# Prompt attention: the scores' float32 products become three products of float32r halves, and ScalarE's order of copies and exponentials is turned round

## The reference, cut to what matters

```python
s = jnp.einsum('nqgrd,nqkgd->nqgrk', qb.astype(jnp.float32), k_g.astype(jnp.float32)) * (HEAD_DIM ** -0.5)
s = jnp.where(valid[:, :, None, None, :], s, -jnp.inf)
p = jax.nn.softmax(s, axis=-1)
o = jnp.einsum('nqgrk,nqkgd->nqgrd', p, v_g.astype(jnp.float32))
```

## Time and profile before

| | |
|---|---|
| median of 3 runs | 2370.66 us (2369.03 to 2371.35) |
| profiled execution, its own time | 2368.82 us |
| its span in the trace | 2365.5 us |
| attention block, first product to last | 491.0 to 662.8 us |
| TensorE, VectorE, ScalarE, GpSimd busy over the span | 95%, 42%, 33%, 27% |

### The profile page before, as it was taken

The page is one execution under the profiler, slowest core; times in us unless marked ns, Lnnn a source line. Parts: engine busy times, 40 slices in busy tenths (PEclk is TensorE's granted clock), DMA queues, the critical chain, the costliest instruction groups (busy, mean ns, idle before and its releaser), DMA issues. The chain is left out here.

```text
span 2365.5 us, 37220 instructions
## 1 busy us (share of the span) xinstructions
PE 2237.6 (95%) x13836; PEld 2057.6 (87%) x13836; DVE 1002.6 (42%) x2441; ACT 781.3 (33%) x1414; POOL 633.8 (27%) x387
## 2 busy tenths in 40 slices
PE   5998899699989999999999999888999999999998
PEld 4885489355579999999999999888999999999998
DVE  2525789776435433333332332457333333323323
ACT  4203578645534312212212212354122122121124
POOL 4110111257735222222222222432222222222224
PEclk8997999789999999999999999899999999999999
DMA  8454373500032111111111111101111111111112
GB/s 304 138 171 123 112 254 117 169 28 1 1 127 80 54 46 45 45 53 44 44 44 44 44 53 54 37 20 45 45 45 45 44 46 51 45 44 44 44 44 82
DMA packets 208668, 170.29 MB, mean 72 GB/s; under 512 B 14477, under 2 KB 202109, under 8 KB 208565
## 3 DMA queue, kind: packets, MB, share of 16 engines
q1 hardware_dynamic: 201917, 154.64, 21.0%
q10 hardware_dynamic: 4160, 8.65, 1.0%
q0 software_dynamic: 2496, 5.77, 1.0%
HBM read 155.85 MB, written 11.64 MB: 71 GB/s over the span
## 5 line engine op out<-in xcount | busy, mean ns | idle before, releaser
L525 PE MATMUL pair<-hhi,whi 128*128 128x352 f32 x2184 | 716.2, 328 | 29.7 <-DVE hlo L726 8.5
L526 PE MATMUL pair<-hlo,whi 128*128 128x352 f32 x2184 | 704.9, 323 | 0.0
L527 PE MATMUL pair<-hhi,wlo 128*128 128x352 f32 x2184 | 704.6, 323 | 0.0
L2193 POOL TENSOR_TENSOR wlo<-wraw,whi 128x1024 fp32r<-128x1024 f32 x127 | 304.4, 2397 | 1145.3 <-ACT whi L2138 1144.1
L525 PE MATMUL pair<-hidh,whi 128*128 128x352 f32 x1536 | 495.4, 323 | 0.0
L526 PE MATMUL pair<-hidl,whi 128*128 128x352 f32 x1536 | 492.7, 321 | 0.0
L527 PE MATMUL pair<-hidh,wlo 128*128 128x352 f32 x1536 | 492.2, 320 | 0.0
L537 DVE SCALAR_TENSOR_TENSOR x<-pair,mod,x 128x352 f32<-128x352 f32 (+1 forms) x432 | 247.3, 573 | 513.6 <-PE pair L527 512.6
L525 PEld LDWEIGHTS pair<-hhi,whi 128*128 128x128 f32 x2184 | 412.4, 189 | 40.7 <-issue 19.2
L526 PEld LDWEIGHTS pair<-hlo,whi 128*128 128x128 f32 x2184 | 413.5, 189 | 0.4
L527 PEld LDWEIGHTS pair<-hhi,wlo 128*128 128x128 f32 x2184 | 412.2, 189 | 0.5
(11 more groups left out here) (287 smaller groups left out, 1964.4 us busy)
## 6 DMA issues: line engine op xcount, KB each, us to landing
wraw<-in_w_up_dram SPq DMA_DIRECT2D x64, 512.0 KB, 3.9
wraw<-in_w_down_dram SPq DMA_DIRECT2D x64, 512.0 KB, 3.4
mraw_i<-in_w_mod_dram SPq DMA_DIRECT2D x20, 1024.0 KB, 5.8
mraw_q<-in_w_mod_dram SPq DMA_DIRECT2D x12, 1024.0 KB, 5.1
mraw<-in_w_mod_dram SPq DMA_DIRECT2D x8, 1024.0 KB, 9.3
wraw<-in_dsa_w_in_dram SPq DMA_DIRECT2D x16, 512.0 KB, 5.9
mraw_w<-in_w_mod_dram SPq DMA_DIRECT2D x8, 1024.0 KB, 5.1
wraw<-in_dsa_w_o_dram SPq DMA_DIRECT2D x16, 512.0 KB, 4.0
```

What stands on the lines that cost most here:

```text
L525: pe.matmul(out, a, hi[:, kr, r], start=(n == 0), stop=False)
L526: pe.matmul(out, a, lo[:, kr, r], start=False, stop=False)
L527: last = pe.matmul(out, b, hi[:, kr, r], start=False, stop=(n == len(ks) - 1))
L2193: pool.tensor_tensor(wlo[:, slot(k), :], wraw[:, slot(k), :], whi[:, slot(k), :], ALU.subtract).then_inc(lo_ready, 1)
```

## The change

The scores of t = 1 to 7 are made of three float32r products (upper query · upper key, upper query · lower key, lower query · upper key) in place of one float32 product. A piece is at least 256 columns wide. For this the halves have to exist: `SPLITS` lists 18 of them (14 of a group of four query heads, 4 of 256 key columns for both key heads, each 128 x 512 elements), placed in rounds h = 1, h = 2 (keys) and h = 4 of the stage before they are used. ScalarE writes the upper half behind the exponential of that round, and VectorE waits for it (`q_upper`) and writes the lower half behind its reciprocal. TensorE waits for `q_rest` at the first head of a group. Tile t = 0 stays as it was. ScalarE's round becomes the copies of n - 3 and then the exponential of n.

```diff
+        KW2 = 2 * P
+        SPLITS = []
+        for t in range(1, TILES):
+            n = HEADS * (t - 1)
+            SPLITS.append((n + 1, "q", t, 0))
+            if t % 2 == 0 or t == 1:
+                SPLITS.append((n + 2, "k", t // 2, None))
+            SPLITS.append((n + 4, "q", t, 1))
+        SPLIT0 = 2 * len(IDX_TILES)
...
+                    if h % GROUP == 0:
+                        pe.wait_ge(q_rest, SPLIT0 + splits_needed(t, h))
+                    a, b = qh[:, t % 2, h, :], ql[:, t % 2, h, :]
                     for s in range((L + 511) // 512):
-                        w = min(512, L - 512 * s)
-                        ins = pe.matmul(pair[1 + n % 2][:, s, 0:w], qt[:, h, t * P:(t + 1) * P],
-                                        kt[:, h // GROUP, 512 * s:512 * s + w], start=True, stop=True)
+                        w = max(KW2, min(512, L - 512 * s))
+                        r = slice(512 * s, 512 * s + w)
+                        out = pair[1 + n % 2][:, s, 0:w]
+                        pe.matmul(out, a, kh[:, h // GROUP, r], start=True, stop=False)
+                        pe.matmul(out, a, kl[:, h // GROUP, r], start=False, stop=False)
+                        ins = pe.matmul(out, b, kh[:, h // GROUP, r], start=False, stop=True)
...
                 for n in range(N + AHEAD):
+                    if n >= AHEAD:
+                        copies(n - AHEAD)
                     if n < N:
                         L = P * (qk_list[n][0] + 1)
                         act.wait_ge(neg_done, n + 1)
...
-                    if n >= AHEAD:
-                        copies(n - AHEAD)
+                    for at_n, kind, i, half in SPLITS:
+                        if at_n == n:
+                            whole, upper, _ = split_parts(kind, i, half)
+                            act.activation(upper, whole, ACT.Copy).then_inc(q_upper, 1)
...
                     if 1 <= n <= N:
                         recip(n - 1)
+                    for m, (at_n, kind, i, half) in enumerate(SPLITS):
+                        if at_n == n:
+                            whole, upper, lower = split_parts(kind, i, half)
+                            dve.wait_ge(q_upper, SPLIT0 + m + 1)
+                            dve.tensor_tensor(lower, whole, upper, ALU.subtract).then_inc(q_rest, 1)
```

More of the change, by code:

```diff
@@ L303, in hybrid_step @@
         pt = [put("pt0", [P, TILES, GROUP * P]), at("pt1", [P, TILES, GROUP * P], F32, whi.manual_sbuf_range[0])]
-        assert pt[0].manual_sbuf_range[1] <= s1 and pt[1].manual_sbuf_range[1] <= wlo.manual_sbuf_range[1]
+        kh, kl = (put(n, [P, KV, SEQ], F32R) for n in ("kh", "kl"))
+        qh, ql = (put(n, [P, 2, HEADS, P], F32R) for n in ("qh", "ql"))
+        assert ql.manual_sbuf_range[1] <= s1 and pt[1].manual_sbuf_range[1] <= wlo.manual_sbuf_range[1]
         pair = [ctx.enter_context(nc.psum_tensor(f"pair{i}", [P, 2, 512], F32)) for i in range(4)]
@@ L1839, in hybrid_step, with split_parts, splits_needed @@
         PV_AFTER = AHEAD + GROUP
+        KW2 = 2 * P
[7 more added lines that the diff above has]
+        SPLIT0 = 2 * len(IDX_TILES)
+        def split_parts(kind, i, half):
+            if kind == "q":
+                h = slice(GROUP * half, GROUP * (half + 1))
+                return qt[:, h, i * P:(i + 1) * P], qh[:, i % 2, h, :], ql[:, i % 2, h, :]
+            c = slice(KW2 * i, KW2 * (i + 1))
+            return kt[:, :, c], kh[:, :, c], kl[:, :, c]
+        def splits_needed(t, h):
+            return max(m for m, (_, kind, i, half) in enumerate(SPLITS)
+                       if (kind == "q" and i == t and half == h // GROUP) or (kind == "k" and i <= t // 2)) + 1
         with nc.Block() as block:
@@ L1856, in qk @@
                     L = P * (t + 1)
-                    for s in range((L + 511) // 512):
-                        w = min(512, L - 512 * s)
-                        ins = pe.matmul(pair[1 + n % 2][:, s, 0:w], qt[:, h, t * P:(t + 1) * P],
-                                        kt[:, h // GROUP, 512 * s:512 * s + w], start=True, stop=True)
+                    if t == 0:
+                        pe.matmul(pair[1 + n % 2][:, 0, 0:P], qt[:, h, 0:P], kt[:, h // GROUP, 0:P], start=True,
+                                  stop=True).then_inc(qk_ready, 1)
+                        return
+                    if h % GROUP == 0:
+                        pe.wait_ge(q_rest, SPLIT0 + splits_needed(t, h))
+                    a, b = qh[:, t % 2, h, :], ql[:, t % 2, h, :]
+                    for s in range((L + 511) // 512):
+                        w = max(KW2, min(512, L - 512 * s))
[4 more added lines that the diff above has]
+                        ins = pe.matmul(out, b, kh[:, h // GROUP, r], start=False, stop=True)
                     ins.then_inc(qk_ready, 1)
```

## The result

The changed kernel takes 2397.49 us (median of 4, 2389.73 to 2398.49), the kernel before 2371.01 us in the same comparison: a ratio of 1.0096, 95% interval 1.0073 to 1.0119. It is slower by about 1%, where 2374.4 us had been forecast with 2381 as the upper end. A second comparison gave 2388.83 against 2371.68 us, ratio 1.0085 (1.0064 to 1.0105).

A forecast was written before the change was run, and what follows sets the result against it. TensorE was taken to bound the block from t = 4 on, VectorE the early stages once halves are added. Stage differences summed to +3.7 us on the 2370.66 us median, giving 2374.4 us, range 2366 to 2381.

The forecast's parts named there:

- The price of a half: On VectorE each half costs the exponential + 0.62 + 0.68 us, 36 us together for the 18.
- the rate of the products: TensorE's float32r score products of 512 columns start 0.23 us apart, saving at most 10.2 us over 8 heads.
- part 3: Stage-by-stage sum over the block: the longer of VectorE's and TensorE's new times sets each stage, +3.7 us.
- clustering: Halves close to the 2 us mask scan stall TensorE: t = 4 to 6 lose up to 1 us each.
- Rival D: TensorE's clock stays at half speed in t = 1 and 2: +4.7 us more, 2379 us; chance 0.10.
- part 4: ScalarE's copies before the exponential end 4.5 us of TensorE waits; nothing gained in VectorE-bound stages.
- B: VectorE's slack hides the halves, so TensorE's saving in t = 4 to 7 comes through: 12.4 us, 2358; chance 0.12.
- C: VectorE's subtraction is held by GpSimd's scaling, 5 us in all, 4 in bound stages: 2378 us; chance 0.12.
- E: Three score products cost as much as two float32 records, 1.02 instead of 0.86 us per 512 columns: 2381; chance 0.08.

The follow-up runs named there:

- e3: The changed kernel with each VectorE subtraction one round later: 2371.06 us, ratio 0.9994 to the kernel before.
- e1: The kernel before with only ScalarE's new order, copies of n - 3 and then exponential of n: 2363.94 us, ratio 0.9968.
- e4: The changed kernel with halves made once ahead of the loops, scores of later tiles left wrong: 2361.56 us, ratio 0.9964.
- e5: The changed kernel with VectorE's reciprocal of the same round moved ahead of the subtraction: 2380.76 us, ratio 1.0064.
- e2: The changed kernel with ScalarE's old order, exponential, copies, then upper half: 2404.38 us, ratio 1.0143.
- f1: Second run of the kernel before with only ScalarE's new order: 2363.42 us, ratio 0.9967.

## Why the prediction was wrong

**What held.** The direction of the argument held: VectorE, not TensorE, sets the early stages, and its waits for ScalarE behind the exponential eat the gain. The price of a half held (23.3 us of waits for 24, 0.69 us for 0.68), as did the stages t = 0 to 2 within 0.5 us and the rate of the products. e3 shows that the waits are the cause, together with all that queues behind them, since nothing else was changed. In the changed kernel's block of +14.8 us, the traces give, one step after the other: order -6.7 (e1), products with halves made ahead -7.2 (e4), the halves back in the loops +6.3 (e3), the waits +22.4 (changed). In another sequence the parts would differ, as the order's 6.7, 9.4 and 18.8 show.

**The step that failed** is part 3, "The longer one sets the stage". I took a stage as the longer of VectorE's list and TensorE's list, with waits on VectorE that only lengthen its own list, and allowed up to 1 us a stage for clustering. The waits cost more than their own length, in t = 3 to 6, in two ways that the longer of two sums cannot show, and a third term was mis-sized. The four stages were forecast at 92.0 us together and took 103.2:

- *The reciprocal.* It stands a round later in VectorE's list, behind the half and the next extraction. GpSimd's scaling starts late, TensorE's turning waits (2.6 to 15.1 us), and the next scores are queued behind it. I named what is queued behind the waiting subtraction as mask step and extraction, and left out the reciprocal of the round itself. e5 moves it and gets 5.9 us of the 11.1 back, two half-speed stretches less included.
- *The clock.* Half-speed stretches in the block grew from 6.8 to 23.9 us, 3.4 of them at 602 after GpSimd's late scalings. Rival D named its sign, a granted clock below 0.9 in t = 1 or 2, and that came true in t = 1 (0.71). The harm it forecast there did not: t = 1 took 12.45 us where VectorE's list alone gives 12.2, and t = 2, at 0.96, took 16.6 and not 20.3. It had not looked at t = 3 and 5 (0.96 and 0.94). It read from the earlier trace rows that the clock stays up through a stretch half busy; here it fell behind one, after 3.83 of 6 us. How much of the block the clock alone costs was not isolated. An estimate of the most it can be in t = 3 to 6: two stretches of 3.4 us in which TensorE did half of what it could, so 3.4 us of the 11.1.
- *The order* of copies and exponentials was counted at nothing of its own in part 4. It is a gain of 6.7 us alone and of 18.8 beside the waits. The forecast used only the share that brings t = 4 to 6 down to TensorE's own time (4.8 us in e1), and said that in the VectorE-bound stages the order brings nothing. There it was wrong: without it t = 0 to 3 take 65.9 us (e2) instead of 61.9. The changed kernel has this gain, so it hid a part of the other two.

Of the remaining 5.2 us (180.1 in e5 against 174.9) 4.7 lie in t = 3 to 6, about 1 us each. That has the size of the clustering that part 3 allowed for at its upper end, in t = 4 to 6; that it is this clustering was not tested.

**Outside the block** the forecast took nothing. The block accounts for 14.8 us. The medians moved by 26.5 and, in the second comparison, 17.2 us. For the kernel with the order alone the traces tell what kind of thing such a rest can be: in e1 the clock was at the lower level from 234 to 265 us, in code that no edit touches, and the block began at 504.6; in its second run (f1) it was not, and the block began at 493.1. PE in e1 (length, busy, granted clock, DMA share, GB/s):

```profile
228.00:234.00 6.00, 3.74 (x24) 1.00 0.90 267
234.00:240.00 6.00, 6.00 (x27) 0.50 0.47 150
```

f1 at the same place:

```profile
228.00:234.00 6.00, 3.94 (x27) 1.00 0.84 259
234.00:240.00 6.00, 5.41 (x38) 1.00 0.50 144
```

Behind the block the rest took 1702.7 to 1709.3 us over all traces. Why three of the four first executions of the changed kernel stood at the low clocks stays open; no trace of one of them exists.

**The rivals.** B fell: e4 shows its saving, but only with the halves taken out. C fell for this kernel: the subtraction took 0.69 us in 17 of 18 cases and 0.81 in one, though 12 began inside a scaling. It is not wrong in general (below). The Trainium skill's rule on ports ("SBUF — State Buffer", section "SBUF: two separate sides") would have held each of the 12. E fell by the 0.23 us distances.

## What to carry to other kernels

A wait put into an in-order list costs its own length and whatever is queued behind it on that engine: write down every instruction of the next round and who waits for each, small ones like a reciprocal above all. When a helper result is needed a whole stage later, consume it a round after its producer, not in the same round; here that one edit was worth 22 us. And add new work for an engine only in the stages where that engine has idle time: halves for three tiles of eight brought more than halves for seven.

## What the runs showed of the hardware that was not expected

**A float32r product behind a float32 one** is recorded as starting 28 ns after the float32 record's start (30 cases of 512 columns in the changed kernel, median), but the next product then starts 0.63 us later instead of 0.23; the pair takes 0.66 us, as 0.43 + 0.23. The row is early, not the work: read the distance over both.

**A VectorE subtraction beside GpSimd's scaling.** Of the 18 in the changed kernel, those that began 0.9 us or more after the start of a scaling took 0.69 us. In e5, where the scaling is released just ahead, eight began 0.05 to 0.27 us after its start, and six of them took more, 0.75 to 1.18 us. The longest, with the scaling beside it:

```profile
585.89 1.18 DVE L2011 TENSOR_TENSOR kl<-kt,kh 128x512 fp32r<-128x512 f32 x1 [0.36 <-ACT kh L1958]
...
585.62 2.66 POOL L1965 TENSOR_SCALAR ss<-ss,small 128x768 f32<-128x768 f32 x1 [1.30 <-DVE small L1972]
```

It ended at 587.07, the scaling at 588.28, so it was slowed or held for a part and not until the scaling's end; the scaling took 2.66 us instead of 2.20. A scaling that began during a subtraction took longer too, and here e5 shows a regular size: at 384, 512 and 640 columns it took 1.71, 1.82 and 1.94 us against 1.24, 1.57 and 1.89, which is 0.47, 0.25 and 0.05 more, where the subtraction had 0.60, 0.39 and 0.18 left (two cases each). So a scaling was held for what was left of the subtraction, less some 0.13 us. For a subtraction that began during a scaling neither "never" nor "for the whole instruction" describes it, and what decides it was not isolated.
